# Keys, values and conv rows stored by channel, and a new order of steps, in a hybrid attention and DeltaNet decoder step

## The chip, the cores and the metric

The kernel runs on one core of a Trainium2 chip. The metric is the device time of one execution in microseconds. Five engines with their own instruction streams matter: TensorE (PE), VectorE (DVE), ScalarE (ACT), GpSimd (POOL), and SyncE (SP), which here only waits and issues DMAs.

## The reference

One layer of a decoder for 512 prompt tokens and 8 decode samples (one token each, 2048 tokens of past). All is float32.

```python
h = rmsnorm(x, g_pre)
q_a, k_a, v_a, z_a, qkv_b, z_b, beta, a = split(h @ w_in)      # 2048 -> 8208 columns
# mixer A, 8 heads x 128: partial rotary (first 32 dims) on q, k; softmax attention under
# (window, dilation) = (128,1), (512,4), (2048,16), the three merged by their denominators
# mixer B, 8 heads: causal conv of width 4 + SiLU on q/k/v, L2 norm, gated delta rule, per-head RMSNorm
gated = concat(o_a * silu(z_a), o_b * silu(z_b))               # 1024 + 1024
y = x + rmsnorm(gated @ w_out, g_post)
# outputs: y (prompt, sample); rotated keys and values of all new tokens; the last 3 conv input
# rows of the prompt; for each sample the old conv rows 1, 2 and the new one; delta states
```

New keys and values are small outputs that nothing else in the layer needs by token, except the values of the prompt, which the attention product takes with tokens on partitions.

## The kernel before

Everything is kept by channel: `h_hi` and `h_lo` hold the 2048 channels of the 520 tokens (512 prompt, 8 samples) as 16 blocks of 128 partitions. A float32 product is made of three products of a faster type: `w_hi h_hi`, `w_hi h_lo`, `w_lo h_hi` (L553 to L555). ACT rounds a weight block to `w_hi` (L954), DVE and POOL make `w_lo` (L1364, L1858), SP loads the next block into `w_raw` (L362) once `w_lo` of the block before it is there.

**Head stretches.** After two first tiles come eight stretches, one per head pair h, of eight projection tiles (q, k, v of mixer B's conv, its gate, then q, k, v, gate of mixer A). The first stretch is written out, the others are a loop; SP writes out the last as well. A tile is computed in two halves (256 and 264 tokens) of four quarters, so a stretch has 64 steps of 12 products. Between two steps every engine runs one step of each side task: Python generators, advanced in the order of a list (`step(work)`). `yield from idle(n)` sets the step at which a piece stands. So the order of each engine is fixed at build time by these numbers and by the order of the list. Side tasks are:
- `own_b`: conv of mixer B's q, k, v (DVE L1521 to L1534), its sigmoid (ACT L970 to L974), the product with it (DVE L1543, keys into `xk`, values into `xv`). The last 3 prompt columns and the 8 sample columns of the conv input `xq` are transposed on PE (L702), copied by ACT (L1178) and stored by two DMAs of ACT's queue.
- `own_a`: rotary on `xa`, `xk` (DVE L1460 to L1462); then PE transposes keys (L650), the sample columns of q and k (L651, L652), values (L657) and their sample columns (L658); ACT copies them to `ktok`, `qkrow`, `vtok`, `vrow` and stores them by token. `scratch_q` passes the sample queries to `qb`, the same row in every partition.
- `mix_b`, `mix_q`: the delta rule in chunks of 128. PE step 24 transposes keys (L715); ACT takes their norms; DVE makes the decay argument (L1554, L1555) and `b_kb` (L1563), which PE transposes at step 28 (L727). At the end PE transposes the output `b_o` (L802) after DVE's L1628.
- `delta_decode`: the samples' step of the delta rule.
- `tail_a(h - 1)`, `attn_decode(h - 1)`: prompt attention and sample attention of the head before. The latter: dot products of the cached keys with `qb` on DVE (L1718), their transposes on PE (L854), softmax on DVE, ACT, DVE (L1727 to L1731, L1269, L1735 to L1740), PE (L858, L860), scaling of the cached values on ACT (L1284), sums on DVE (L1743, L1746), column sums on PE (L865).

**After the last head** come 40 more steps with the output projection's first tiles (L887 to L889): each step is four blocks k of one half. Their input, the gated rows of the 16 head halves, was kept in DRAM (`scratch_g`) and is read back: rows 0 to 8 early, 9 to 14 by `late_rows`, in groups that share a semaphore (`ROW_GROUPS`). `splits(n)` names the rows that ACT (`g_hi`, L1311) and DVE (`g_lo`, L1767) split at step n: rows 8, 9 at n = 2, rows 10, 11 at n = 3. The tail and decode of the last head run in the same steps. Then a part follows in which DVE adds output tiles (L1799 to L1804), and then 11 plain tiles.

Of the kernel before, what the change touches and what calls it, by code (L numbers as in the profile page):

```python
# [6 lines left out]
F32 = mybir.dt.float32  # L7
# [5 lines left out]
P = 128  # L13
# [119 lines left out]
ROW_GROUPS = ((0, 1, 2, 3, 4, 5, 6, 8), (9, 10, 11), (12, 13, 14))  # L133
# [38 lines left out]
def build(nc, x_prompt, x_sample, cache_k, cache_v, state_conv, state_delta, g_pre, w_in, w_ba, conv_w, a_log, dt_bias,  # L172
          onorm_w, w_out, g_post, c_ident, c_upper, c_causal, c_levels, c_lnmask, c_rope,
          y_p, y_s, wk_p, wv_p, cv_p, st_p, wk_s, wv_s, cv_s, st_s):
    kp_v = wk_p[0, 0].rearrange("(c p) h d -> p c h d", p=P)
    vp_v = wv_p[0, 0].rearrange("(c p) h d -> p c h d", p=P)
    scratch_q = nc.dram_tensor("scratch_q", (NH, NB * HD), F32, kind="Internal").ap()
    scratch_g = nc.dram_tensor("scratch_g", (KT, P, TP), F32, kind="Internal").ap()

    with ExitStack() as ctx:  # L180
# [3 lines left out]
        def sem(name):  # L184
# [22 lines left out]
        ktok = mem[:, 15 * TP:16 * TP].rearrange("p (c d) -> p c d", c=NC)  # L207
# [44 lines left out]
        qkrow = rb[0:NB, 5 * P:7 * P].rearrange("p (n t) -> p n t", n=2)  # L252
        vrow = rb[0:NB, 7 * P:8 * P]
# [57 lines left out]
        def mx(n):  # L311
# [10 lines left out]
            "q_swap q_ok k_swap k_ok k_T ktok_ok k_out v_T vtok_ok v_out row_out qrow_out scores negmax expd "  # L322
# [4 lines left out]
            "zero_cols cw_ok crow_ps crow_ok crow_out conv_ok conv_sig kv_silu q_silu "  # L327
# [29 lines left out]
        def _(sp):  # L357
# [37 lines left out]
            sp.dma_start(cv_s[0, :, 0:2, :], state_conv[0, :, 1:3, :]).then_inc(s["S_out"], 16)  # L395
# [22 lines left out]
            def attn_decode(hh):  # L418
                yield from idle(8)
# [11 lines left out]
            def attn_rows(h):  # L431
# [9 lines left out]
                sp.dma_start(qb[:], scratch_q[h].partition_broadcast(P)).then_inc(s["qb_in"], 16)  # L441
# [25 lines left out]
            def early_rows():  # L467
# [3 lines left out]
                for k in (4, 5):  # L471
                    load_row(k)
# [45 lines left out]
            sp.wait_ge(s["h_lo_ok"], H_READY + KT + 2)  # L518
            for c in range(NC):
# [22 lines left out]
        def _(pe):  # L542
# [99 lines left out]
            def own_a(h):  # L642

                yield from idle(53)
                pe.wait_ge(s["k_ok"], h + 1)
                pe.wait_ge(s["d_add"], 2 * h + 2)
# [4 lines left out]
                pe.transpose(MD[0:NB, 1, 0:P], xa[:, TP:TT], ident[:])  # L651
                pe.transpose(MD[0:NB, 1, P:2 * P], xk[:, TP:TT], ident[:]).then_inc(s["k_T"], 1)  # L652
                yield from idle(6)
                pe.wait_ge(s["proj_sb"], 16 * h + 16)
# [1326 lines left out]
```

## Time and profile before

| | us |
|---|---|
| median of 3 runs | 1336.98 (1335.55 to 1337.41) |
| the profiled execution | 1335.67 |
| its span | 1333.8 |
| PE busy | 1255.9 (94%) |
| DVE busy | 768.1 (58%) |
| ACT busy | 543.2 (41%) |
| POOL busy | 288.6 (22%) |
| mean granted clock of PE | 0.988 |

Busy time of PE counts each product from its start to its end, and they overlap; so what an instruction costs is read from the starts of its neighbours. The granted clock is a share of 2.4 GHz. A difference between two times of this kernel below 0.2% can't be told from none.

### The profile page before, as it was taken

To read this page: it belongs to the slowest core of one execution; us is meant where nothing else is said; L and a number is where in the kernel's file an instruction comes from. 1 tells how busy PE (TensorE), PEld (TensorE's weight loads), DVE (VectorE), ACT (ScalarE), POOL (GpSimd) and SP (SyncE) were. 2 spreads that over 40 slices of the span, in tenths; PEclk is the share of its full clock that TensorE was granted. 3 is DMA by queue.
4 is the path that set the end of the run, shared out by engine and by line. 5 is a ranking of instruction groups with operands and counts; after the bars stand their busy time and mean duration, and the time that the engine had idled before them with its cause. 6 is when DMAs were issued, how large, how long until landed. Compare 5 with 4: busy or idle time off the path is not lost. (4 is left out here: it accounts for less than half of the span.)

```text
span 1333.8 us, 28478 instructions
## 1 busy us (share of the span) xinstructions
PE 1255.9 (94%) x10094; PEld 1208.7 (91%) x10094; DVE 768.1 (58%) x1872; ACT 543.2 (41%) x1472; POOL 288.6 (22%) x271
## 2 busy tenths in 40 slices
PE   4999998999999999999999999999999998899997
PEld 4989998999899989998999899989998997889996
DVE  6465377537653775376537753765377555474445
ACT  6353344434443444334433443344334544412210
POOL 1123212321232123112321231123212311122220
PEclk9999999999999999999999999999999998999999
DMA  7231434143424342434243424342434254312253
GB/s 227 90 96 50 145 108 140 61 142 101 130 66 140 98 135 66 138 103 129 64 140 100 133 66 138 105 127 65 138 100 150 66 184 130 110 64 94 94 190 129
DMA packets 82707, 151.90 MB, mean 114 GB/s; under 512 B 8793, under 2 KB 27330, under 8 KB 81026
## 3 DMA queue, kind: packets, MB, share of 16 engines
q1 hardware_dynamic: 72222, 144.87, 33.7%
q10 hardware_dynamic: 10384, 5.50, 1.6%
q8 instruction: 86, 1.41, 0.4%
q14 instruction: 15, 0.12, 0.0%
HBM read 132.20 MB, written 17.27 MB: 112 GB/s over the span
## 5 line engine op out<-in xcount | busy, mean ns | idle before, releaser
L553 PE MATMUL PJ<-h_hi,w_hi 128*128 128x264 f32 (+1 forms) x2432 | 722.4, 297 | 7.7 <-ACT memx L981 7.6
L554 PE MATMUL PJ<-h_lo,w_hi 128*128 128x264 f32 (+1 forms) x2432 | 688.2, 283 | 0.0
L555 PE MATMUL PJ<-h_hi,w_lo 128*128 128x264 f32 (+1 forms) x2432 | 686.6, 282 | 0.0
L553 PEld LDWEIGHTS PJ<-h_hi,w_hi 128*128 128x128 f32 x2432 | 461.0, 190 | 25.5 <-issue 12.4
L554 PEld LDWEIGHTS PJ<-h_lo,w_hi 128*128 128x128 f32 x2432 | 461.0, 190 | 2.8 <-issue 1.7
L555 PEld LDWEIGHTS PJ<-h_hi,w_lo 128*128 128x128 f32 x2432 | 459.2, 189 | 0.0
L1858 POOL TENSOR_TENSOR w_lo<-w_raw,w_hi 128x512 fp32r<-128x512 f32 x160 | 210.3, 1314 | 897.4 <-ACT w_hi L954 897.4
L954 ACT ACTIVATE w_hi<-w_raw 128x512 fp32r<-128x512 f32 x320 | 197.6, 624 | 103.2 <-PE PJ L555 84.1
L1364 DVE TENSOR_TENSOR w_lo<-w_raw,w_hi 128x512 fp32r<-128x512 f32 x160 | 114.0, 718 | 117.1 <-ACT w_hi L954 113.4
L981 ACT ACTIVATE memx<-PJ 128x264 f32<-128x264 f32 (+2 forms) x130 | 49.2, 380 | 68.4 <-PE PJ L555 57.0
L1223 ACT ACTIVATE mem<-MX 128x256 f32<-128x256 f32 x48 | 18.4, 384 | 116.1 <-PE MX L755 115.5
L1601 DVE TENSOR_TENSOR mem<-mem,MX 128x256 f32<-128x256 f32 (+1 forms) x48 | 18.9, 395 | 75.2 <-PE MX L774 75.2
L1523 DVE SCALAR_TENSOR_TENSOR memx<-memx,cw 128x512 f32<-128x512 f32 x72 | 60.4, 839 | 1.7
L887 PE MATMUL PJ<-h_hi,w_hi 128*128 128x256 f32 (+1 forms) x160 | 50.2, 314 | 7.9 <-DVE h_lo L1767 4.9
L1718 DVE CUSTOM_DVE_ANT_0 kv<-kv,qb 128x128 f32<-128x128 f32 x192 | 51.2, 323 | 0.0
L1907 POOL TENSOR_TENSOR mem<-mem,levels 128x256 f32<-128x256 f32 x48 | 38.8, 809 | 49.8 <-DVE mem L1576 22.0
L888 PE MATMUL PJ<-h_lo,w_hi 128*128 128x256 f32 (+1 forms) x160 | 47.2, 295 | 0.0
L889 PE MATMUL PJ<-h_hi,w_lo 128*128 128x256 f32 (+1 forms) x160 | 47.0, 294 | 0.0
L1801 DVE COPY memx<-PJ 128x256 f32<-128x256 f32 (+1 forms) x24 | 10.3, 428 | 63.0 <-PE PJ L555 61.8
L774 PE MATMUL MX<-mem 128*128 128x64 f32 x352 | 45.0, 269 | 0.0
L774 PEld LDWEIGHTS MX<-mem 128*128 128x128 f32 x352 | 43.1, 192 | 0.0
L1284 ACT ACTIVATE kv<-kv,pT 128x128 f32<-128x128 f32 x128 | 40.4, 389 | 4.5 <-issue 4.5
(317 smaller groups left out, 1618.4 us busy)
## 6 DMA issues: line engine op xcount, KB each, us to landing
w_raw<-in_w_in SPq DMA_DIRECT2D x256, 256.0 KB, 2.6
w_raw<-in_w_out SPq DMA_DIRECT2D x64, 256.0 KB, 2.8
kv<-in_cache_win_k SPq DMA_DIRECT2D x24, 512.0 KB, 3.5
kv<-in_cache_win_v SPq DMA_DIRECT2D x16, 512.0 KB, 3.5
mem<-in_x_prompt SPq DMA_DIRECT2D x4, 1024.0 KB, 10.1
S<-in_state_delta SPq DMA_DIRECT2D x8, 512.0 KB, 3.4
out<-S SPq DMA_DIRECT2D x8, 512.0 KB, 3.8
out<-mem ACTq DMA_DIRECT2D x16, 256.0 KB, 3.2
```

Of the source, the lines that this page charges most:

```text
L553: pe.matmul(out, wh, h_hi[:, k, tok], start=k == 0, stop=False)
L554: pe.matmul(out, wh, h_lo[:, k, tok], start=False, stop=False)
L555: last = pe.matmul(out, wl, h_hi[:, k, tok], start=False, stop=k == KT - 1)
L774: last = pe.matmul(blocks(mx(3)[:, c, :], n, c // 2), b_U[:, c, :], blocks(b_Y[:, c % 2, :], n, c // 2), start=True, stop=True)
L887: pe.matmul(out, wh, h_hi[:, k, tok], start=start and i == 0, stop=False)
L888: pe.matmul(out, wh, h_lo[:, k, tok], start=False, stop=False)
L954: act.activation(w_hi[:, par, 4 * q:4 * q + 4, :], w_raw[:, q, :, :], ACT.Copy).then_inc(s["w_hi_ok"], 1)
L981: act.activation(dst[:, o:o + WIDTH[half]], PJ[0:n, bank(T, half), 0:WIDTH[half]], ACT.Copy).then_inc(s["proj_sb"], 1)
L1364: dve.tensor_tensor(w_lo[:, par, 4 * q:4 * q + 4, :], w_raw[:, q, :, :], w_hi[:, par, 4 * q:4 * q + 4, :].bitcast(F32), ALU.subtract).then ...
L1523: link(dve.scalar_tensor_tensor(acc[:, 0:TP], xq[:, i:i + TP], w[:, 24 + i:25 + i], acc[:, 0:TP], ALU.mult, ALU.add))
L1718: last = dve.tensor_tensor_reduce(out=x, in0=x, in1=qb[:, b * HD:(b + 1) * HD], scale=1.0, scalar=0.0, op0=ALU.mult, op1=ALU.add, accum_ou ...
L1858: pool.tensor_tensor(w_lo[:, par, 4 * q:4 * q + 4, :], w_raw[:, q, :, :], w_hi[:, par, 4 * q:4 * q + 4, :].bitcast(F32), ALU.subtract).the ...
```

## The change

1. Keys, values, conv rows and sample queries are stored by channel, straight from `xk`, `xv`, `xq`, `xa`, by SP (`conv_out`, `attn_out`). The outputs of the program have other shapes; the host puts their axes in order. PE's transposes L650, L651, L652, L658 and L702 and ACT's copies and stores of them go. The transposes of the prompt's values stay, one step later. Guards on `xq`, `xk`, `xv` now wait for the stores.
2. On DVE, `mix_b` comes before `own_b` and `own_a` in the list of the loop.
3. In the loop, `attn_decode` runs its softmax part two steps later (`late=2`) on DVE, PE, ACT; the value scaling and the sums keep their steps.
4. Row 9 gets the place of `ktok` and is reloaded with rows 4 and 5. After the last head SP runs a step of its side tasks before the weight load of that step, not behind it.
5. The last head's `attn_decode` runs six steps sooner (`late=-6`) on all engines.

```diff
-ROW_GROUPS = ((0, 1, 2, 3, 4, 5, 6, 8), (9, 10, 11), (12, 13, 14))
+ROW_GROUPS = ((0, 1, 2, 3, 4, 5, 6, 8, 9), (10, 11), (12, 13, 14))
...
+            def conv_out(h):
+                yield from idle(9)
+                for j in range(3):
+                    sp.wait_ge(s["proj_sb"], 16 * h + (2 * j + 4))
+                    sp.dma_start(c_new[h, j], xq[:, TP:3 + TT]).then_inc(s["crow_out"], 16)
+                    yield from idle(8)
+            def attn_out(h):
+                yield from idle(46)
+                sp.wait_ge(s["q_ok"], h + 1)
+                sp.dma_start(scratch_q[h], xa[:, TP:TT]).then_inc(s["qrow_out"], 16)
+                yield from idle(7)
+                sp.wait_ge(s["k_ok"], h + 1)
+                sp.dma_start(k_new[h], xk).then_inc(s["k_out"], 16)
+                yield from idle(5)
+                sp.wait_ge(s["proj_sb"], 16 * h + 16)
+                sp.dma_start(v_new[h], xv).then_inc(s["v_out"], 16)
...
-                for k in (4, 5):
+                for k in (4, 5, 9):
                     load_row(k)
...
             def late_rows():
                 sp.wait_ge(s["gated_b"], NH)
-                for k in (9, 10, 11):
+                for k in (10, 11):
                     load_row(k)
                 yield
                 sp.wait_ge(s["v_T"], NH)
                 sp.wait_ge(s["stash_v"], NH)
+                sp.wait_ge(s["v_out"], 16 * NH)
                 for k in (12, 13, 14):
                     load_row(k)
...
-            work = [late_rows(), attn_decode(h)]
+            work = [late_rows(), attn_decode(h, late=-6)]
             for n in range(40):
+                step(work)
                 if n % 2 == 0 and n < 8 * PARTS:
                     slot, p = n // 8, n // 2 % 4
                     wait_lo(T_O + slot + 1, p)
                     load_out(slot + 2, p)
-                step(work)
...   PE
             def own_a(h):
-                yield from idle(53)
...
+                yield from idle(60)
+                pe.wait_ge(s["proj_sb"], 16 * h + 16)
                 if not isinstance(h, int) or h > 0:
                     pe.wait_ge(s["gated_ad"], h)
                 for c in range(NC):
-                    pe.transpose(MD[:, 0, c * P:(c + 1) * P], xk[:, c * P:(c + 1) * P], ident[:])
...
-            def own_b(h):
-                for j in range(3):
-                    yield from idle((11, 7, 8)[j])
...
-                    pe.transpose(MD[0:11, 1, 0:P], xq[:, 3 + TP - 3:3 + TT], ident[:]).then_inc(s["crow_ps"], 1)
...   ACT, guard of the copy into xq
                     act.wait_ge(s["conv_ok"], 3 * h + n)
-                    act.wait_ge(s["crow_ps"], 3 * h + n)
+                    act.wait_ge(s["crow_out"], 16 * (3 * h + n))
...   DVE
-                stretch(h, [tail_a(h - 1), attn_decode(h - 1, sums=(24, 4, 3)), own_b(h), own_a(h), mix_b(h), mix_q(h),
+                stretch(h, [tail_a(h - 1), attn_decode(h - 1, late=2, sums=(22, 4, 3)), mix_b(h), own_b(h), own_a(h), mix_q(h),
                             delta_decode(h)])
```

What moves on DVE, in the loop, around step 25: `memx<-memx,cw` are the conv of q, `mem<-MX,hg` and `mem<-mem,causal` the decay argument, the first `mem<-MX,sk` is `b_kb`. Before:

```order
L1364 TENSOR_TENSOR w_lo<-w_raw,w_hi 128x512
L1523 SCALAR_TENSOR_TENSOR memx<-memx,cw 128x512
L1523 SCALAR_TENSOR_TENSOR memx<-memx,cw 128x512
...
L1534 TENSOR_SCALAR memx<-memx 128x520
L1554 TENSOR_TENSOR mem<-MX,hg 128x512
L1555 SCALAR_TENSOR_TENSOR mem<-mem,causal 128x512
L1563 TENSOR_TENSOR mem<-MX,sk 128x512
```

In the changed kernel, whose lines have other numbers:

```order
L1325 TENSOR_TENSOR w_lo<-w_raw,w_hi 128x512
L1517 TENSOR_TENSOR mem<-MX,hg 128x512
L1518 SCALAR_TENSOR_TENSOR mem<-mem,causal 128x512
L1484 SCALAR_TENSOR_TENSOR memx<-memx,cw 128x512
L1484 SCALAR_TENSOR_TENSOR memx<-memx,cw 128x512
...
L1495 TENSOR_SCALAR memx<-memx 128x520
L1526 TENSOR_TENSOR mem<-MX,sk 128x512
```

The decay argument moved ahead of the end of the conv; the same instructions stand between the weight step and `b_kb`.

On PE at steps 59 and 60 of a stretch (`ident,memx` are transposes of values, `ident,mem` that of `b_o`). Before:

```order
L555 MATMUL PJ<-h_hi,w_lo 128x256
L657 MATMUL MD<-ident,memx 128x128 [waits ktok_ok,proj_sb]
L657 MATMUL MD<-ident,memx 128x128 x3
L658 MATMUL MD<-ident,memx 8x128
L802 MATMUL MX<-ident,mem 128x128 [waits o_n]
L802 MATMUL MX<-ident,mem 128x128 x3
L553 MATMUL PJ<-h_hi,w_hi 128x264 [waits proj_sb]
```

And now:

```order
L797 MATMUL MX<-ident,mem 128x128 [waits o_n]
L797 MATMUL MX<-ident,mem 128x128 x3
L568 MATMUL PJ<-h_hi,w_hi 128x264 [waits proj_sb]
...
L570 MATMUL PJ<-h_hi,w_lo 128x264
L664 MATMUL MD<-ident,memx 128x128 [waits proj_sb]
L664 MATMUL MD<-ident,memx 128x128 x3
```

The value transposes moved from ahead of `b_o` to 12 products behind it.

On SP after the last head (`w_raw` are weight loads, `mem` and `memx<-scratch_g` the gated rows, `kv` cached keys). Before:

```order
L362 DMA w_raw<-in_w_out 128x512 [waits w_lo_dve]
L465 DMA mem<-scratch_g 128x512 [waits gated_b]
L465 DMA mem<-scratch_g 128x512 x2
L465 DMA mem<-scratch_g 128x512 [waits stash_v,v_T]
L465 DMA memx<-scratch_g 128x512 x2
L362 DMA w_raw<-in_w_out 128x512 [waits w_lo_pool]
```

And now:

```order
L479 DMA mem<-scratch_g 128x512 [waits gated_b]
L479 DMA mem<-scratch_g 128x512
L356 DMA w_raw<-in_w_out 128x512 [waits w_lo_dve]
L479 DMA mem<-scratch_g 128x512 [waits v_out,stash_v,v_T]
L479 DMA memx<-scratch_g 128x512 x2
L511 DMA out<-small 128x128
L415 DMA kv<-in_cache_win_k 128x1024 [waits red]
L356 DMA w_raw<-in_w_out 128x512 [waits w_lo_pool]
```

Two rows stand ahead of the weight load that waits for DVE, and a load of cached keys, which waits for the first dot products, stands ahead of the next.

## Rows read from the trace of the kernel before

**Rows 1.** The page: busy time of TensorE and its share, the other engines beside it.

```profile
PE 1255.9 (94%) x10094; PEld 1208.7 (91%) x10094; DVE 768.1 (58%) x1872; ACT 543.2 (41%) x1472; POOL 288.6 (22%) x271
```

**Rows 2.** Waits of all engines (waiter, releaser: us in total, times, longest).

```profile
PE MX L727 <- DVE mem L1563: 19.6, 8, 2.6
...
ACT rb L1269 <- DVE ds L1731: 12.9, 8, 1.6
...
PE MD L854 <- DVE sc L1718: 5.9, 7, 0.8
...
PE PJ L887 <- DVE h_lo L1767: 4.9, 2, 3.8
...
PE MD L865 <- DVE kv L1746: 4.6, 1, 4.6
...
PE MD L858 <- DVE rb L1740: 4.4, 7, 0.6
...
PE PJ L887 <- DVE mem L1802: 2.9, 2, 2.0
```

**Rows 3.** Three stretches: busy us and (instructions) by engine, then granted clock, DMA share, GB/s.

```profile
350.00:360.00 10.00, 7.57 (x52) 7.54 (x52) 4.92 (x10) 5.40 (x12) 2.55 (x2) 0.83 0.29 90
1108.00:1119.00 11.00, 8.34 (x35) 6.50 (x35) 7.56 (x14) 3.95 (x10) 1.27 (x1) 0.69 0.22 80
1160.00:1170.00 10.00, 8.32 (x44) 8.32 (x45) 5.07 (x14) 2.02 (x5) 1.28 (x1) 0.66 0.13 37
```

**Rows 4.** Timeline of PE around one conv row: start us, us, instruction.

```profile
348.25 0.28 PE L555 MATMUL PJ<-h_hi,w_lo 128*128 128x256 f32 x1
348.37 0.27 PE L702 MATMUL MD<-ident,memx 128*11 128x128 f32 x1
...
348.60 0.27 PE L554 MATMUL PJ<-h_lo,w_hi 128*128 128x256 f32 x1
```

**Rows 5.** Timeline of PE at step 53 of the last head.

```profile
1079.53 0.60 PE L650 MATMUL MD<-ident,memx 128*128 128x128 f32 x4
...
1080.18 0.39 PE L781 MATMUL MX<-small,mem 128*128 128x128 f32 x2
```

**Rows 6.** Timeline of PE at step 59 of a head ([idle before <-releaser] last).

```profile
291.95 0.60 PE L657 MATMUL MD<-ident,memx 128*128 128x128 f32 x4
...
292.82 0.66 PE L802 MATMUL MX<-ident,mem 128*128 128x128 f32 x4 [0.15 <-DVE mem L1628]
```

**Rows 7.** Timeline of VectorE (DVE) ahead of `b_kb`, same head as rows 4.

```profile
346.55 0.69 DVE L1364 TENSOR_TENSOR w_lo<-w_raw,w_hi 128x512 fp32r<-128x512 f32 x1 [1.03 <-ACT w_hi L954]
...
350.85 0.69 DVE L1555 SCALAR_TENSOR_TENSOR mem<-mem,causal 128x512 f32<-128x512 f32 x1
...
351.72 0.69 DVE L1563 TENSOR_TENSOR mem<-MX,sk 128x512 f32<-128x512 f32 x1
```

**Rows 8.** Timeline of all engines before L715, same head.

```profile
339.07 0.43 DVE L1534 TENSOR_SCALAR memx<-memx 128x520 f32<-128x520 f32 x1
...
342.58 0.69 DVE L1543 TENSOR_TENSOR memx<-memx 128x520 f32<-128x520 f32 x1
...
344.22 0.49 PE L715 MATMUL MX<-ident,memx 128*128 128x128 f32 x3
```

**Rows 9.** DMA issues: KB each, median us from issue to landing.

```profile
mem<-scratch_g SPq DMA_DIRECT2D x8, 256.0 KB, 4.5
...
memr<-memx ACTq DMA_DIRECT2D x32, 32.5 KB, 2.1
```

**Rows 10.** Timeline of SyncE's queue after the last head.

```profile
1095.30 6.44 SPq L362 DMA_DIRECT2D w_raw<-in_w_out  x3
1101.78 2.21 SPq L465 DMA_DIRECT2D mem<-scratch_g  x4
```

**Rows 11.** Timeline of ScalarE (ACT) and PE at the end of the last decode.

```profile
1154.47 2.44 ACT L1284 ACTIVATE qb<-qb,pT 128x128 f32<-128x128 f32 x8
...
1161.68 3.48 PE L865 MATMUL MD<-ones,kv 128*128 128x1 f32 x16 [4.65 <-DVE kv L1746]
```

More of the change, by code:

```diff
@@ L416, in stretch, with attn_decode @@
                 over(work)
-            def attn_decode(hh):
-                yield from idle(8)
+            def attn_decode(hh, late=0):
+                yield from idle(8 + late)
                 sp.wait_ge(s["red"], 3 * hh + 1)
@@ L649, in own_a @@
                 for c in range(NC):
-                    pe.transpose(MD[:, 0, c * P:(c + 1) * P], xk[:, c * P:(c + 1) * P], ident[:])
[L651 to L654, printed above, removed]
-                pe.wait_ge(s["ktok_ok"], 2 * h + 2)
-                for c in range(NC):
-                    pe.transpose(MD[:, 0, c * P:(c + 1) * P], xv[:, c * P:(c + 1) * P], ident[:])
-                pe.transpose(MD[0:NB, 1, 0:P], xv[:, TP:TT], ident[:]).then_inc(s["v_T"], 1)
+                    last = pe.transpose(MD[:, 0, c * P:(c + 1) * P], xv[:, c * P:(c + 1) * P], ident[:])
+                last.then_inc(s["v_T"], 1)
             def tail_a(hh):
@@ L845, in delta_decode, with attn_decode @@
                               stop=True).then_inc(s["d_outer"], 1)
-            def attn_decode(hh, sums=12):
-                yield from idle(17)
-                pe.wait_ge(s["vtok_ok"], 2 * hh + 2)
+            def attn_decode(hh, late=0, sums=12):
+                yield from idle(17 + late)
+                pe.wait_ge(s["vtok_ok"], hh + 1)
                 pe.wait_ge(s["qkp"], hh + 1)
@@ L890, in unit @@
                 return last
-            work = [later(tail_a(NH - 1)), attn_decode(NH - 1)]
+            work = [later(tail_a(NH - 1)), attn_decode(NH - 1, late=-6)]
             for n in range(40):
@@ L1171, in own_b @@
             def own_b(h):
-                for j, m in enumerate((1, 2, 0)):
-                    yield from idle((11, 4, 5)[j])
-                    act.wait_ge(s["crow_ps"], 3 * h + j + 1)
-                    if j > 0 or not isinstance(h, int) or h > 0:
-                        act.wait_ge(s["crow_out"], 32 * (3 * h + j))
-                    act.activation(rows, MD[0:11, 1, 0:P], ACT.Copy).then_inc(s["crow_ok"], 1)
-                    yield
+                for j in range(3):
+                    yield from idle((12, 5, 6)[j])
                     act.wait_ge(s["conv_ok"], 3 * h + j + 1)
@@ L1261, in delta_decode, with attn_decode @@
                     s["d_rows_ok"], 1)
-            def attn_decode(hh, lag=0, gap=0):
-                yield from idle(18)
-                act.wait_ge(s["row_out"], 16 * hh + 16)
-                act.wait_ge(s["qrow_out"], 16 * hh + 16)
-                act.wait_ge(s["v_out"], 32 * hh + 32)
+            def attn_decode(hh, late=0, lag=0, gap=0):
+                yield from idle(18 + late)
                 act.wait_ge(s["sc_max"], hh + 1)
@@ L1323, in _ @@
             g_hi_samples(0, KT - 1)
-            work = [later(tail_a(NH - 1)), attn_decode(NH - 1)]
+            work = [later(tail_a(NH - 1)), attn_decode(NH - 1, late=-6)]
             for n in range(40):
@@ L1708, in bt_s, with attn_decode @@
                 return dd[:, 12 - n, :]
-            def attn_decode(hh, sums=(9, 1, 4)):
-                yield from idle(7)
+            def attn_decode(hh, late=0, sums=(9, 1, 4)):
+                yield from idle(7 + min(late, 0))
                 dve.wait_ge(s["qb_in"], 16 * hh + 16)
+                q = qb[:].rearrange("p (d b) -> p b d", b=NB)
                 for n in range(3):
@@ L1723, in attn_decode @@
                     last.then_inc(s["red"], 1)
-                yield
-                yield
+                yield from idle(2 + max(late, 0))
                 dve.wait_ge(s["sc_T"], hh + 1)
@@ L1777, in _ @@
             g_lo_samples(0, KT - 1, 5)
-            work = [later(tail_a(NH - 1)), attn_decode(NH - 1)]
+            work = [later(tail_a(NH - 1)), attn_decode(NH - 1, late=-6)]
             for n in range(40):
@@ L1979 @@
     r = run_bass_kernel_spmd(nc, [arrays], core_ids=[0])
[L1980 removed]
+    return tuple(np.ascontiguousarray(a) for a in outputs(*(r.results[0][f"out_{i}"] for i in range(len(_OUTS)))))
```

99 lines of the change are left out of this document (34 added, 65 removed).

## The prediction

> **What bounds the kernel now.** I read the page's engine shares first. TensorE (PE) is busy in 94% of the span [rows 1], and no other engine is above 58%, so an edit is worth what it takes off PE's own instruction stream, or off a wait that PE really sits in. The list of waits comes second [rows 2]: PE's waits inside the eight head stretches are 19.6 us before the transpose of `b_kb` (L727, 2.45 on average, in each of 8 heads), 5.9 before L854 and 4.4 before L858 (7 heads each, decode softmax of the head before). After the stretches come 4.9 for `h_lo`, 4.6 for L865 and 2.9 for L1802. Third is the granted clock [rows 3]: it falls from 2.4 to 1.2 GHz after such waits. In 350 to 360 us the mean is 0.83, so 10 x 0.17 = 1.7 us are lost; three of the eight heads (3, 5 and 7) show this fall. In 1108 to 1119 it is 11 x 0.31 = 3.4 us, in 1160 to 1170 also 3.4. So the rest of the prediction asks, for each edit, whether PE then arrives earlier at the next wait or really finishes earlier.
>
> **Transposes that go.** Ten per head: three of conv rows (L702), four of keys and two of decode rows (L650 to L652), one of the decode value row (L658). Their busy time is no price, since PE overlaps them: around L702 the product two places on starts at 348.60 where it would have started 0.236 after 348.25 without it, at 348.49, so one costs 0.11 us [rows 4]. The six of step 53 take from 1079.53 to 1080.18, 0.65 us [rows 5]. All 80 are 8 x (0.65 + 0.44) = 8.7 us of stream. How much is kept depends on what PE meets next.
> - The six of step 53: nothing that PE waits for follows within the next steps, all 0.65 is kept. 8 x 0.65 = 5.2 us.
> - The value row and the four value transposes stood directly ahead of L802 and covered its wait for `b_o`. PE starts them at 291.95 and L802 at 292.82, still with 0.15 idle [rows 6]. The end of that wait is set by DVE and ACT, counted from L798. In the changed order L802 comes first and the value transposes one step (12 products) later. So L802 ends where it ended, the row's 0.11 buys nothing, and four transposes are paid anew: 4 x 0.11 plus about 0.08 for the broken stream, 0.52 per head, 4.2 us lost. Bounds: 0 (if `b_o` is ready earlier) and 0.87 - 0.15 = 0.72 per head.
> - The conv rows of steps 11, 18 and 26 lie in the stretch where DVE is behind PE (below). I give them nothing; the bound is 24 x 0.11 = 2.6 us.
>
> **"Mixer steps lead" on DVE.** L727 waits for L1563. The order rows show what the lead does: L1554 and L1555 now come before the last conv pieces instead of behind them, but L1563 is a step later and keeps all of the same work ahead of it. From the weight step at 346.55 DVE runs without a gap to L1563's end at 352.41 [rows 7]; a permutation of that row of instructions ends at the same time. The wait stays. It even grows by the 0.11 of the conv transpose that PE no longer runs in between, and by the 0.2 of the small ACT copy `pT`, which now comes in front of the weight copy that DVE waits for: 8 x 0.3 = 2.4 us more idle, of which 0.9 is only the saving that isn't kept. Net 1.5 us lost. What does come earlier is ACT's L1215, and PE waits for nothing behind it. I leave three clock falls in heads as they are; from none to eight they are worth -5 to +8.5 us.
>
> **Decode softmax two steps later.** L854 then finds its sums ready: 0.84 x 7 = 5.9 us gone. But DVE is the late one there, and what it owes is shifted. Before: conv end (L1534) at 339.07 to 339.50, then six small softmax operations, the weight step, and the value product L1543 from 342.58 to 343.27, with PE's L715 free to start at 344.22 [rows 8]. After: L1534 is 1.2 us earlier (the five L1727 to L1731 operations come behind it, to 339.3), ACT follows with its sigmoid, the exponentials and the weight copy until about 341.1, DVE with the weight step (341.8), the six softmax operations (343.05) and L1543 (343.75). L858 and L860 (0.45 us) now stand right ahead of L715. So PE would reach L858 at about 342.1, wait till 343.1, and start L715 at about 343.8: 0.4 us earlier than before, not the 0.84 + 0.62 that the two waits add up to. 7 x 0.4 = 2.8 us; bounds -0.3 (nothing but the two columns' cost) and 1.5 per head. ACT loses 24 small copies and eight pairs of large and small ones; PE's stream waits for none of them.
>
> **SP's new DMAs.** Six small or medium stores per head move from ACT's queue to SP's (0.33 us of issue each) and stand among weight loads. None of the values they wait for is later than the `w_lo` that SP has just waited for, so the loads behind them are late by about 2 us in a head where each has a tile (11 us) to spare. New is that `xq` may be overwritten only when its store has landed. The tightest store stands at step 17 and the overwriting copy on ACT at step 20, three steps of 12 x 0.118 = 1.4 us [rows 4], 4.2 us, against 2.1 us to landing for a 32.5 KB copy and 4.5 for a 256 KB row [rows 9]. I price it at 0 (bounds 0 to 1 us per head; PE asks for that copy some four steps later).
>
> **After the last head.** Here is the gain. Rows 9 to 14 leave SP at 1101.78, behind the last of three weight loads, which waits for DVE [rows 10], and PE stands 3.8 and 1.1 us for their `h_lo` [rows 2]. In the changed order row 9 comes with the early ones and rows 10, 11 leave before that load, at about 1098 (the load before it and 0.5 of issue), and land near 1102.5 by the 4.5 us of such rows [rows 9]; PE asks for them from 1106 on. The waits go (4.9 us), and the fall of the clock goes (3.4 us) [rows 3]. The first dot products of the last decode now sit on DVE between rows 7 to 11 (8 x 0.21 = 1.7 us), so about 1 us of new small waits comes back. The last decode itself: ACT scales values until 1156.91, DVE adds till 1161.6, and PE, out of other work for 4.65 us, runs L865 at half clock (3.48 us instead of 1.7) [rows 11]. Six steps sooner and with a chain that starts about 8 us sooner, I get by the same durations: dots done 1119.6, L854 at step 11, L858 at 1129.6, ACT's scaling 1130.4 to 1140.4, sums by 1144, and step 28 of PE ends at 1147.3. The wait goes (4.6), L865 takes 1.7 (1.8 saved), and the next 2.8 us of products at half clock give back 1.4. Sum: 4.9 + 3.4 + 4.6 + 1.8 + 1.4 - 1.0 = 15.1 us. Bounds: 8 us (only the rows' waits and their clock, less the dots) and 18 (with the 2.9 us before L1802 as well).
>
> **Sum.** 5.2 - 4.2 - 1.5 + 2.8 + 15.1 = 17.4 us, from 1335.67 us of the profiled execution (span 1333.8, 1.9 around it): 1318.3. The median of the runs shown (1336.98) is 1.3 above that execution, so 1319.5.
>
> **Rivals.**
> - *Slower: the softmax ahead of the value product holds every head.* L1543 now stands behind operations that wait for ACT's exponentials, and L715, the weight step and L1563 stand behind L1543. If ACT takes `p_exp` later than I laid out (it now lies behind two sigmoid passes), L715 is late in each of seven heads, and its idle time brings the clock down each time (1.7 us). For it: PE waits for DVE at two places of this stretch already. Against: ACT stood idle 12.9 / 8 = 1.6 us before that very operation [rows 2]. It decides from 17.4 / 7 = 2.5 us per head lost against the forecast, or from 1.3 us with falls in all eight heads; with 1.9 us and the falls it is 1319.5 + 13.3 + 8.5 = 1341.
> - *Half of the tail.* The dots between the row splits, or V loads that wait for `red`, hold PE up again and the clock falls once more: 8 instead of 15.1, 1326.6. For it: DVE, ACT and SP are all denser there than anywhere before. Falls of the clock in all eight heads alone end at 1328.
> - *The transposes count in full.* `b_o` is ready earlier, or PE is late enough everywhere that conv rows, value row and moved values cost and give as listed: 8.7 us where the forecast keeps 5.2 - 4.2 - 1.5 = -0.5: 1310.3.
> - *The lead does what its name says*, L727's wait vanishes with its clock falls: 19.6 + 5 us more than forecast, 1295. Against it stands the row of instructions itself. A rule of the Trainium skill comes out in the same place: "TensorE: Matmul & The Clock Gate", Part 4, counts about 275 ns for a transpose in a kernel. By that rule 80 are 22 us, 22.5 more than the forecast, and the sum would be 1297; the trace agrees with it as a duration (272 ns), while the starts lie 0.11 us apart.
>
> **How the numbers follow.** Forecast 0.55 (own range 1313 to 1323), full transposes 0.13, half of the tail 0.17, the lead 0.07, slower rival 0.08. The range 1307 to 1327 holds the first three but for their edges and leaves out some 0.16. A difference of 0.2% is what a measurement of this kernel can tell. Faster by more: 0.91; the slower rival splits into 0.03 within 0.2% and 0.06 slower.
>
> **What would show it.** Right: PE's wait before the `b_kb` transpose is still there, 2.5 to 2.9 us in eight heads; the wait before the `b_o` transpose grows from 0.15 to about 0.7; no wait before the scores' small transposes; no PE gap between the stretch's end and the first projection tile's third part; the last value sums end before PE's step 28. Wrong: heads (132.9 us apart now, from the first L802 to the last) shorter by over 1.5 us or longer by over 0.5; the wait for `b_kb` below 1 us; a new wait of PE for `h_lo` above 2 us.

## The result and the profile after

The changed kernel takes 1344.99 us (median of 4 runs, 1344.43 to 1345.91) against 1336.26 of the kernel before in the same comparison: a ratio of 1.0064 with a 95% interval of 1.0045 to 1.0083. It is slower, and 25.5 us above the forecast of 1319.5. The profiled run has a span of 1342.8.

The first view is the mean clock, one row of each kernel. By an estimate, 1342.8 x 0.019 = 25.5 us are lost to the lower level after and 1333.8 x 0.012 = 16.0 before; the part of it that falls into PE's own waits costs nothing.

```profile
core 0: 1333.8 us, clock 0.988
```

```profile
core 0: 1342.8 us, clock 0.981
```

The next view splits both spans at the first and the last transpose of `b_o` (L802 before, L797 after). In a row stand the length, the busy time with its instructions of PE, PEld, DVE, ACT and POOL, the clock, DMA share and GB/s.

```profile
161.70:1092.20 930.50, 894.20 (x7227) 859.43 (x7228) 549.68 (x1407) 406.98 (x1156) 212.08 (x204) 0.99 0.35 111
1092.20:1333.80 241.60, 221.87 (x1729) 213.82 (x1727) 130.30 (x299) 64.05 (x136) 42.21 (x33) 0.95 0.35 121
```

```profile
160.10:1110.50 950.40, 899.82 (x7157) 866.49 (x7158) 573.73 (x1407) 393.05 (x1113) 215.10 (x204) 0.98 0.35 109
1110.50:1342.80 232.30, 217.82 (x1733) 210.83 (x1731) 134.35 (x299) 63.99 (x135) 43.19 (x33) 0.98 0.37 126
```

The seven distances between heads (from one `b_o` transpose to the next) grew by 19.9 us together (132.9 to 135.8 each). What follows the last head shrank from 241.6 to 232.3, by 9.3. DVE is busy 24 us more in the heads although it has the same 1407 instructions: some of them got slower. The waits of PE after, answering to [rows 2]:

```profile
PE MX L722 <- DVE mem L1526: 19.7, 8, 3.6
...
PE MD L853 <- DVE rb L1703: 12.7, 7, 1.8
PE PJ L568 <- ACT memx L976: 10.5, 8, 1.6
PE MD L849 <- DVE sc L1682: 6.8, 8, 1.9
PE MX L797 <- DVE mem L1591: 5.6, 8, 0.7
```

Two of before that [rows 2] leaves out:

```profile
PE PJ L553 <- ACT memx L981: 7.6, 7, 1.4
...
PE MX L802 <- DVE mem L1628: 1.2, 8, 0.2
```

The five waits of the heads are 19.6 + 5.9 + 4.4 + 7.6 + 1.2 = 38.7 us before, and 19.7 + 12.7 + 10.5 + 5.6 and 4.9 of L849's 6.8 (1.9 fall behind the heads) = 53.4 after: 14.7 more. The ten transposes give 7 x 1.1 = 7.6 back. The other 13 of the 19.9 us fit the clock: by the estimate above its loss grew by 9.5 in all, though the part behind the heads lost 241.6 x 0.05 = 12 before and 232.3 x 0.02 = 5 after, so the heads lost some 16 more.

The wait for `b_kb` (L722 now) is where it was. The one for `b_o` (L797) is 0.70 in each of 8 heads, as forecast. The scores' wait (L849) did not go, and that for `rb` (L853) is three times what it was. The waits for `h_lo` and for the last value sums [rows 2, 11] are gone. But 11.6 us behind the last `b_o` PE makes a new stop:

```profile
1121.69 0.39 PE L882 MATMUL PJ<-h_hi,w_hi 128*128 128x264 f32 x1 [2.33 <-issue]
```

"Issue" means that the trace names nothing that PE waited for. Most kernels below have this stop too, at 1.5 to 3.3 us, also the two without the new order behind the heads (1.7 and 1.8); the kernel before has none. Its cause stays open. Two further views name what made DVE slow. First one line of DVE, the dot products of the decode: minimum, median and maximum in ns.

```profile
L1718 DVE CUSTOM_DVE_ANT_0 kv<-kv,qb x192: 276/283/1380, 183.1 to 1136.4; 128x128 f32<-128x128 f32 x192
```

```profile
L1682 DVE CUSTOM_DVE_ANT_0 kv<-kv,qb x192: 371/405/1510, 181.9 to 1142.3; 128x128 f32<-128x128 f32 x192
```

Second, the timeline of DVE and POOL ahead of L853, in the head of [rows 8], and a piece of the kernel before:

```profile
347.07 0.69 DVE L1325 TENSOR_TENSOR w_lo<-w_raw,w_hi 128x512 fp32r<-128x512 f32 x1 [1.86 <-ACT w_hi L949]
...
348.03 0.15 DVE L1700 RECIPROCAL ds<-ds 8x1 f32<-8x1 f32 x1
348.17 1.27 POOL L1819 TENSOR_TENSOR w_lo<-w_raw,w_hi 128x512 fp32r<-128x512 f32 x1 [10.01 <-ACT w_hi L949]
348.22 1.22 DVE L1701 TENSOR_TENSOR ds<-ds 8x1 f32<-8x1 f32 x1
...
349.48 0.22 DVE L1702 TENSOR_SCALAR dg<-ident,ds 8x8 f32<-8x8 f32 x1
349.62 0.40 DVE L1703 TENSOR_SCALAR rb<-rb,ds 8x384 f32<-8x384 f32 x1
...
350.07 0.38 PE L853 MATMUL MD<-dg,ones 8*128 8x8 f32 x2 [1.83 <-DVE rb L1703]
```

```profile
337.72 1.28 POOL L1858 TENSOR_TENSOR w_lo<-w_raw,w_hi 128x512 fp32r<-128x512 f32 x1 [6.03 <-ACT w_hi L954]
337.76 1.27 DVE L1531 SCALAR_TENSOR_TENSOR memx<-memx,cw 128x8 f32<-128x8 f32 x1
```

L1701 is a product of two 8x1 operands and takes 0.147 us elsewhere. Here it starts 0.05 us after POOL's `w_lo` and ends with it. In the kernel before, the POOL instruction of this stretch fell on L1531, a small piece of the conv ahead of these six operations.

### The profile page after: what moved, and what is told of

Same layout as the page of the kernel before. It is cut to its first block and busy times, and to the rows that moved or that the text cites. A ratio compares the mean times of both kernels' runs of the same rounds, so it can differ in the third digit from the quotient of the medians.

```text
span 1342.8 us, 28094 instructions
## 1 busy us (share of the span) xinstructions
PE 1255.2 (93%) x10014; PEld 1210.8 (90%) x10014; DVE 796.1 (59%) x1872; ACT 527.6 (39%) x1424; POOL 292.2 (22%) x271
## 2 busy tenths in 40 slices
DMA packets 80252, 151.80 MB, mean 113 GB/s; under 512 B 12945, under 2 KB 22834, under 8 KB 78578
## 3 DMA queue, kind: packets, MB, share of 16 engines
q10 hardware_dynamic: 1024, 1.07, 0.3%
## 5 line engine op out<-in xcount | busy, mean ns | idle before, releaser
L568 PE MATMUL PJ<-h_hi,w_hi 128*128 128x264 f32 (+1 forms) x2432 | 725.9, 298 | 10.5 <-ACT memx L976 10.5
L1819 POOL TENSOR_TENSOR w_lo<-w_raw,w_hi 128x512 fp32r<-128x512 f32 x160 | 214.7, 1344 | 890.7 <-ACT w_hi L949 890.7
L1682 DVE CUSTOM_DVE_ANT_0 kv<-kv,qb 128x128 f32<-128x128 f32 x192 | 76.6, 456 | 0.0
L965 ACT ACTIVATE memx<-memx 128x520 f32<-128x520 f32 x32 | 20.4, 636 | 138.4 <-DVE memx L1495 138.4
L1868 POOL TENSOR_TENSOR mem<-mem,levels 128x256 f32<-128x256 f32 x48 | 35.7, 743 | 58.1 <-DVE mem L1539 30.4
```

The lines of the kernel that those rows point to most:

```text
L568: pe.matmul(out, wh, h_hi[:, k, tok], start=k == 0, stop=False)
L1682: last = dve.tensor_tensor_reduce(out=x, in0=x, in1=q[:, b, :], scale=1.0, scalar=0.0, op0=ALU.mult, op1=ALU.add, accum_out=sc[:, n, b:b + 1])
L1819: pool.tensor_tensor(w_lo[:, par, 4 * q:4 * q + 4, :], w_raw[:, q, :, :], w_hi[:, par, 4 * q:4 * q + 4, :].bitcast(F32), ALU.subtract).the ...
```

## The experiments

A difference between two experiments is one of medians; where the intervals of their ratios overlap the text says so. The ratios are to the kernel before, run beside each (its medians were 1336.3 to 1338.6).

**Queries by token, written by the DMA itself.** The dot products read `qb[:].rearrange("p (d b) -> p b d", b=NB)`: 128 numbers, each 8 elements behind the last. That line stands in the change's code; my prediction gave it no term, and the diff above does not show it.

```diff
-sp.dma_start(scratch_q[h], xa[:, TP:TT])
+sp.dma_start(scratch_q[h].rearrange("(b d) -> d b", b=NB), xa[:, TP:TT])
...
-in1=q[:, b, :]
+in1=qb[:, b * HD:(b + 1) * HD]
...
```

> The changed kernel, but the sample queries lie by token in DRAM again, so that the dot products of the decode read qb with step 1 and not with step 8. Theory 1, the step: the 192 dots fall from 0.405 to 0.283 us, DVE is 24 x 0.12 = 2.9 us earlier in each head, the wait before L853 falls from 1.8 to under 0.8 us, the extra clock falls in the heads go, heads come down from 135.8 to about 132.5 us, the time to 1345.0 - 7 x 3.3 - 1 = 1321 (1316 to 1326). Theory 2, the order (softmax ahead of the value product, list order): DVE's dots get faster but DVE then waits for ACT in the same place, the wait before L853 stays near 1.8 us and the time stays above 1338.

Measured: 1370.18 (ratio 1.025, 1.0224 to 1.0275). Both theories missed. The dots fell to 0.285, but the store now consists of 1024 pieces of 4 bytes, and the small DMAs that swap the rotary rows were late:

```profile
DVE memx L1421 <- DMA memr<-memx: 39.0, 8, 8.0
...
PE MX L776 <- DVE small L1579: 24.4, 8, 5.9
```

DVE's rotary waits up to 8.0 us for the swapped rows of `xk`, and PE sits behind it at L776, where the changed kernel has no such wait. The two kernels derived from this one share that fault.

> As q_by_token, with the last decode at its old steps and SP's side tasks behind the weight load again (row 9 stays with the early rows). Theory 1 (the tail gains what its waits and clock falls show, 9 to 15 us): 9 to 15 us above q_by_token, near 1333, and the wait for the last value sums (4.6 us) is back. Theory 2 (the tail's gain is given back by DVE's denser steps): within 4 us of q_by_token.

Measured: 1376.98 (1.0282 to 1.0332), 6.8 above `q_by_token`; under the range of theory 1, over that of theory 2. It is measured again below without the fault.

> As q_by_token, with the softmax of the decode in the loop at its old steps (late=0, sums back). Theory 1 (my forecast's step: later is worth 0.4 us per head): 7 x 0.4 = 2.8 us above q_by_token. Theory 2 (the six operations ahead of the value product L1506 hold PE): 3 us or more below q_by_token, since the value product comes earlier. Theory 3 (DVE's work is only permuted): the same within 1.5 us.

Measured: 1360.74 (1.0144 to 1.0203), 9.4 below `q_by_token`: theory 2's direction. In the profiled executions the difference is 3.0 (1367.37 and 1364.39).

**The step alone, in the kernel before.** The dots read `in1=qb[:].rearrange("p (d b) -> p b d", b=NB)[:, b, :]`; nothing else differs.

> The kernel before, where only the dot products read qb with step 8; the scores are then made of the wrong elements, all else is computed as before. Theory 1: dots of 0.4 us, DVE 2.9 us later at the end of them, the waits before L854 and L727 grow by 2 to 3 us together in each head, with clock falls behind them: 1336.3 + 7 x 3 = 1357 (1350 to 1364). Theory 2: the dots have slack in the old order, under 0.5 us per head: 1336 to 1340.

Measured: 1353.24 (1.0128, 1.0103 to 1.0152), 16 us slower, by theory 1. The wait for the scores grew from 5.9 to 15.3 us and that for `b_kb` stayed; the clock (0.982) took some 8 more, by the same estimate.

```profile
PE MX L727 <- DVE mem L1563: 19.6, 8, 2.7
PE MD L854 <- DVE sc L1718: 15.3, 7, 2.2
```

**The step alone, in the changed kernel.** One line, so that the dots read with step 1.

```diff
-q = qb[:].rearrange("p (d b) -> p b d", b=NB)
+q = qb[:].rearrange("p (b d) -> p b d", b=NB)
```

> The changed kernel with nothing changed but the view through which the dot products read qb, step 1 in place of 8; the scores are then made of the wrong elements, and the store by channel and its DMA stay. Theory 1 (the reading step is the whole difference between the changed kernel and q_via_pe): dots of 0.283 us, 1329.3 - 0.9 (8 transposes of 0.11 less) = 1328.4 (1325 to 1331). Theory 2 (part of it was the DMA of the queries on SP's queue): 1335 or more.

Measured: 1333.35 (0.9956, 0.9935 to 0.9977). The step costs 11.6 us by the medians and 14 by the two ratios to the kernel before. The time is between the two theories.

**Queries by token through PE.** One transpose at step 53, one ACT copy, a store in full rows: 8 x 0.11 us of PE more, step 1, no pieces of 4 bytes. The main lines:

```diff
+pe.transpose(MD[0:NB, 1, 0:P], xa[:, TP:TT], ident[:])
...
+act.activation(rb[0:NB, 5 * P:6 * P], MD[0:NB, 1, 0:P], ACT.Copy)
...
+act.dma_start(scratch_q[h].rearrange("(b d) -> b d", b=NB), rb[0:NB, 5 * P:6 * P])
```

> The changed kernel, but the sample queries are transposed by PE at step 53, copied by ACT and stored by token in full rows, so that qb is read with step 1 and no DMA of 4-byte elements goes out. Theory 1 (step 8 is the whole loss): dots of 0.283 us, the wait before L722 and L853 back at their sum of before, 1321 (1316 to 1326). Theory 2 (two causes: step 8, and POOL's w_lo, which runs from 348.17 to 349.44 and keeps L1701 until it ends, in front of L853): the wait before the scores' small transposes stays at 1.8 us in each of 7 heads, only the wait for L976 (0.6 of 1.3 us) and a few clock falls go: 1332 to 1340.

Measured: 1329.34 (0.9945, 0.9923 to 0.9968). The time lies between the two ranges; the wait is theory 2's. That for `rb` is as it was after, 12.7 us:

```profile
PE MX L723 <- DVE mem L1538: 21.6, 8, 3.6
...
PE MD L855 <- DVE rb L1714: 12.7, 7, 1.8
```

This kernel has all the rest of the change, so what is left of the forecast's miss is read from it.

**Softmax at its old steps** (`late=0` in the loop on DVE, PE, ACT; the sums and the value scaling keep their steps), on `q_via_pe` and on the changed kernel.

> As q_via_pe, with the decode's softmax in the loop at its old steps. Theory 2 (there POOL's w_lo falls on conv pieces and not on the six small operations): the wait for rb falls from 1.8 to 0.6 us, 7 x 1.2 and clock falls less: 7 to 12 us below q_via_pe, near 1326. My forecast's step (later is worth 0.4 us a head): 2.8 us above q_via_pe. Theory 3 (a permutation): the same within 1.5 us.

> The changed kernel with the decode's softmax in the loop at its old steps, qb still read with step 8. Theory 2: the dots are late for L849 (wait 0.8 to 2.2 us, as in before_q_step8), the wait for rb falls to 0.6: both causes are of like size, so the time stays within 5 us of the changed kernel (1340 to 1348). If the six small operations were the larger cause by far, it falls below 1338; if step 8 alone counted, it rises above 1350.

Measured: 1326.42 (0.9912, 0.9881 to 0.9943), 2.9 below `q_via_pe`, and 1345.56 (1.0056), the same as the changed kernel. The second agrees with theory 2. The first has its direction at under half its price of 7 to 12, and the intervals of the ratios overlap; the two profiled executions differ by 0.4 us. So the time alone doesn't exclude theory 3. PE's waits in the heads even add up to the same: 21.6 + 12.7 + 6.2 = 40.5 us in `q_via_pe`, 27.2 + 7.4 + 5.1 + 1.2 = 40.9 here. What differs is where PE stands in a head. Its `b_o` and `b_kb` transposes in `q_via_pe`, then with the softmax at its old steps:

```profile
296.38 0.66 PE L798 MATMUL MX<-ident,mem 128*128 128x128 f32 x4 [0.70 <-DVE mem L1603]
357.85 0.66 PE L723 MATMUL MX<-ident,mem 128*128 128x128 f32 x4 [2.04 <-DVE mem L1538]
```

```profile
296.03 0.66 PE L798 MATMUL MX<-ident,mem 128*128 128x128 f32 x4 [0.70 <-DVE mem L1603]
356.38 0.65 PE L723 MATMUL MX<-ident,mem 128*128 128x128 f32 x4 [3.49 <-DVE mem L1538]
```

The distance is 61.47 us with the late softmax and 60.35 without, and within 0.03 the same in the next three heads; the key transposes between them stand 0.96 us later with it. The clock takes most of these 1.1 us back. Stretches of 10 us ahead of `b_kb` and behind it in `q_via_pe`, in the head above and in one with a longer wait:

```profile
347.50:357.80 10.30, 7.90 (x53) 7.61 (x53) 8.73 (x18) 4.58 (x19) 1.28 (x1) 0.83 0.37 125
357.80:368.00 10.20, 10.15 (x86) 10.16 (x86) 4.98 (x10) 3.98 (x8) 2.21 (x2) 1.00 0.21 64
613.40:623.70 10.30, 6.36 (x53) 6.07 (x53) 8.72 (x18) 4.58 (x19) 1.26 (x1) 0.95 0.40 123
623.70:634.00 10.30, 10.29 (x65) 10.29 (x66) 2.54 (x4) 3.34 (x7) 1.28 (x1) 0.72 0.17 63
```

Where the clock is down ahead of `b_kb` (0.83), PE arrives late at a wait that it would have anyway (2.04 us), and behind it the clock is at its upper level. Where it falls behind `b_kb` (0.72), PE has waited 3.56 us and the fall costs stream. Of the seven heads of the loop, `q_via_pe` has four of the first kind and three that wait 3.56 with the fall behind; with the softmax at its old steps all seven wait 3.5 and have it behind (1.00 ahead, 0.83 behind). What sets this stays open.

**Is it POOL?** The two small tensor_tensor operations as tensor_scalar; then POOL's `w_lo` of step 22 behind the softmax.

```diff
...
-dve.tensor_tensor(ds[:, 4:5], ds[:, 4:5], ds[:, 5:6], ALU.mult)
+dve.tensor_scalar(ds[:, 4:5], ds[:, 4:5], ds[:, 5:6], None, ALU.mult)
```

> As q_via_pe, with the two small tensor_tensor operations of the softmax's second part (sum and product, 8x1) written as tensor_scalar with the second number as a scalar operand. If POOL holds back only DVE operations with two tensors read from SBUF, L1701 falls from 1.22 to 0.15 us, the wait for rb from 1.8 to about 0.75, and the time by 7 x 1.07 to 7 x 1.07 + 6 (clock falls): 8 to 13 us below q_via_pe. If POOL holds back every DVE operation that starts while it runs, or the 1.07 us has another cause, nothing changes (within 1.5 us), or the wait moves to the next operation.

Measured: 1336.27 (0.9982, 0.9961 to 1.0003), 7 us slower (the intervals just overlap). DVE and POOL, with times from the start of the span:

```profile
347.08 1.26 POOL L1830 TENSOR_TENSOR w_lo<-w_raw,w_hi 128x512 fp32r<-128x512 f32 x1 [9.64 <-ACT w_hi L951]
...
347.19 0.20 DVE L1712 TENSOR_SCALAR ds<-ds 8x1 f32<-8x1 f32 x1
347.43 0.95 DVE L1713 TENSOR_SCALAR dg<-ident,ds 8x8 f32<-8x8 f32 x1
```

The product is held no more, but the next operation is, until POOL ends. The wait for `rb` fell from 1.81 to 1.57, and that for `b_kb` grew from 21.6 to 26.8 us. The mean clock is 0.980 against 0.988, some 11 us. Six heads wait 3.58 us for `b_kb` here, the second kind above, where `q_via_pe` has three; why a shift of 0.25 us brings that many, I can't say.

```diff
+if j == 2 and seg == 6 and not isinstance(h, int):
+    pool.wait_ge(s["p_norm"], h)
```

> q_via_pe, where POOL's w_lo of step 22 in the loop waits until DVE has made the last of the six small operations of the softmax. Theory 1 (POOL's operation holds DVE's L1712 for 1.07 us, and this is in front of PE): L1712 falls from 1.23 to 0.15 us, the wait for rb from 1.8 to 0.75, 7 x 1.07 and some clock falls: 1318 to 1323. Theory 2 (what is gained there is lost again at the next wait, b_kb, as with q_via_pe_one_input, since POOL then holds the conv pieces ahead of it): the wait for b_kb grows by as much, within 2 us of q_via_pe (1329.3), or slower.

Measured: 1326.65 (0.9913, 0.9892 to 0.9935), 2.7 below `q_via_pe`; the intervals overlap. L1712 is 0.147 in all 8 heads, so the 1.07 us are POOL's. The time is 0.7 below theory 2's range and 3.7 above theory 1's, and the waits are theory 2's:

```profile
PE MX L723 <- DVE mem L1538: 27.7, 8, 3.6
...
PE MD L855 <- DVE rb L1714: 5.1, 7, 0.8
```

7.6 us went from the wait for `rb` and 6.1 came back in front of `b_kb`. The transposes of `b_kb` do come earlier:

```profile
295.95 0.66 PE L798 MATMUL MX<-ident,mem 128*128 128x128 f32 x4 [0.70 <-DVE mem L1603]
356.29 0.66 PE L723 MATMUL MX<-ident,mem 128*128 128x128 f32 x4 [3.56 <-DVE mem L1538]
```

That is 60.34 us against 61.47, the same place as with the softmax at its old steps. So POOL's operation accounts for the whole 1.1 us that the two later steps cost there, and again the clock falls behind `b_kb` in all seven heads of the loop, which fits that only 2.7 us are left of 7 x 1.1.

**List order of before** (`mix_b` behind `own_b` and `own_a`), on `q_via_pe_late0`.

> q_via_pe_late0 with the list order of before on DVE (own_b, own_a ahead of mix_b). Theory 1 (my forecast: the lead only permutes DVE's row ahead of b_kb): the wait for b_kb stays near 3.4 us and the time within 2 us of q_via_pe_late0 (1326.4). Theory 2 (the lead has a cost of its own: POOL's w_lo now falls on a conv piece in front of b_kb, 1.0 us): the wait falls to about 2.4 us, and the time by 8 x 1 = 8 us and some clock falls, 1310 to 1318.

Measured: 1322.93 (0.9891, 0.9861 to 0.9920), 3.5 below; the ratios overlap, the waits don't: 27.2 us for `b_kb` with the lead, 20.5 without. The `b_kb` transposes stand 59.38 us behind those of `b_o` instead of 60.35. DVE and POOL with the lead, then without:

```profile
353.28 1.44 DVE L1504 SCALAR_TENSOR_TENSOR memx<-cw,memx 128x8 f32<-128x8 f32 x2
353.44 1.26 POOL L1830 TENSOR_TENSOR w_lo<-w_raw,w_hi 128x512 fp32r<-128x512 f32 x1 [5.96 <-ACT w_hi L951]
...
355.63 0.69 DVE L1538 TENSOR_TENSOR mem<-MX,sk 128x512 f32<-128x512 f32 x1
```

```profile
349.39 0.49 DVE L1504 SCALAR_TENSOR_TENSOR memx<-cw,memx 128x8 f32<-128x8 f32 x2
...
352.12 0.69 DVE L1538 TENSOR_TENSOR mem<-MX,sk 128x512 f32<-128x512 f32 x1
...
353.85 1.29 POOL L1830 TENSOR_TENSOR w_lo<-w_raw,w_hi 128x512 fp32r<-128x512 f32 x1 [8.92 <-ACT w_hi L951]
```

With the lead, ACT gets its decay argument sooner, so its weight copy and with it POOL's `w_lo` start sooner, and POOL lands on a conv piece (1.44 for two instead of 0.49) ahead of `b_kb`. Without, it comes behind `b_kb`. Theory 2 by its wait; the time is between the two ranges, at under half of theory 2's price.

**Value transposes at step 59.**

> q_via_pe_late0 with PE's four value transposes at step 59 again, directly ahead of those of b_o. My forecast's step (they cover the wait for b_o and are paid anew behind it): the wait for b_o falls from 0.70 to about 0.2 us, 8 x 0.5 = 4 us below q_via_pe_late0, 1322.5. Rival (their place is free, DVE sets the end of each head anyway): the same within 1.5 us.

Measured: 1321.85 (0.9883, 0.9855 to 0.9910), 4.6 below; the ratios overlap, and the wait for `b_o` is 0.26 in each head instead of 0.70. As forecast.

**The tail undone**, on `q_via_pe`.

> q_via_pe with the last decode at its old steps and SP's side tasks behind the weight load again (row 9 stays early). Theory 1 (my forecast's 15.1 us of the tail, of which row 9 alone is some 2): 9 to 15 us above q_via_pe, 1338 to 1345, with a wait for the last value sums near 4.6 us. Theory 2 (most of the gain is row 9 and the clock): within 5 us, up to 1334.

Measured: 1336.95 (0.9988, 0.9972 to 1.0005), 7.6 above, between the two ranges; 4.7 us of wait for the last value sums are back. A wait for `h_lo` is not, so the early place of row 9, which stays here, is enough to remove those 4.9 us. In the profiled executions the part behind the last `b_o` is 226.1 us with the edits (the row of `q_via_pe` below, at full clock) and 237.9 without. But 226.1 is the shortest of all: in the eleven profiled kernels with these edits and fast dots it goes up to 229.8, with 228.2 in the middle.

```profile
1098.40:1324.50 226.10, 214.39 (x1733) 206.10 (x1731) 130.03 (x299) 63.82 (x135) 43.11 (x33) 1.00 0.38 130
```

**`b_kb` sooner.** None of the above moves `b_kb` ahead of the conv's end. One `yield` does:

```diff
 dve.scalar_tensor_tensor(b_D, ...).then_inc(s["mix_arg"], 1)
-yield
 dve.wait_ge(s["mix_rs"], 2 * h + 1)
...
 dve.tensor_tensor(b_kdec, mx(0), ...)
+yield
 yield
```

> q_via_pe_late0, but DVE makes b_kb in the same step as the decay argument (step 25), ahead of the end of the conv, instead of one step later. Theory 1 (b_kb is late only because of the conv pieces and POOL's lock in front of it, 3.9 us): the wait of 3.4 us in each of 8 heads goes, and with it most clock falls in heads: 27 + 5 to 10 us below q_via_pe_late0, 1290 to 1297. Theory 2 (the conv then ends 1.5 us later and the wait turns up behind it, at ACT's sigmoid, at b_A or at the next b_o): half of it or less, 1310 to 1326.

> late0_kb_sooner with the value transposes at step 59 ahead of those of b_o (the two gains together). Theory 1, they add: 1310.8 - 4.6 = 1306 (1303 to 1309), the wait for b_o at 0.26 us. Theory 2, DVE sets the head's end anyway: 1310.8 within 1.5 us.

The first measured 1310.75 (0.9796, 0.9768 to 0.9823), 15.7 below `q_via_pe_late0`: the wait for `b_kb` is gone but in the written-out first head, and 15.1 us turned up behind it, two steps on, where PE waits for ACT's copy of the transposed `b_kb` (theory 2). The second, with the value transposes at step 59, measured 1302.91 (0.9734, 0.9712 to 0.9756), 7.9 further down, so the two gains add (theory 1, 0.1 under its range). In that comparison the kernel before took 1338.6, so it is 36 us faster, and the fastest of all. Its rows:

```profile
PE MX L729 <- ACT mem L1193: 15.2, 7, 2.2
...
PE MX L723 <- DVE mem L1537: 2.8, 1, 2.8
...
PE MX L798 <- DVE mem L1603: 2.1, 8, 0.3
```

```profile
162.00:1074.20 912.20, 881.12 (x7164) 849.71 (x7165) 549.34 (x1407) 394.90 (x1122) 212.59 (x204) 1.00 0.36 113
1074.20:1300.40 226.20, 213.36 (x1729) 205.46 (x1727) 129.42 (x299) 63.36 (x135) 43.19 (x33) 1.00 0.38 130
```

## Why the prediction was wrong

The steps of the prediction against what was measured, from the bottom of its sum:

- **The missing term.** DVE's 192 dots read `qb` with step 8 and take 0.405 us, not 0.283: 24 x 0.12 = 2.9 us more for DVE in each head. The prediction left this at nothing: it took the durations of DVE's row from the trace of before for operations whose operand had a new layout, in the heads and behind them (8 x 0.21 for the first dots of the last decode, which now start 0.34 us apart). Alone this costs 11.6 to 14 us in the changed kernel and 16 in the one before. A rule of the Trainium skill speaks of it: "SBUF — State Buffer", Door 1, says that a float32 operand may step by up to 4 elements for free and pays beyond. The measured 43% on the whole instruction at step 8 agree in sign; the Trainium skill gives no price for DVE there.
- **"L715 starts 0.4 us earlier", the softmax two steps later.** Forecast 2.8 us gained; measured 2.9 lost by medians whose intervals overlap. In the traces the key transposes stand 0.96 us later in each head, and those of `b_kb` 1.1. The prediction let L1735 to L1740 take 1.25 us by the rows of before. At their new step POOL's `w_lo` runs beside them and holds one for 1.07 us; with POOL behind them the 1.1 us are gone. The place was the slower rival's (the softmax in front of the value product), the mechanism not: that rival blamed ACT's exponentials, so that its 1341 lies near the 1345 measured is luck.
- **"A permutation of that row ends at the same time."** Forecast 1.5 us lost beside; measured 3.5 more by the lead (its ratios overlap), with `b_kb` 0.97 us later in each head. The sum of DVE's durations is not kept when the order changes, since it depends on what POOL does meanwhile. The Trainium skill, "SBUF — State Buffer", "SBUF: two separate sides", has the rule: DVE and GpSimd share one port pair under an exclusive lock; a DVE operation with two SBUF inputs or in a 2-port mode and a GpSimd operation block each other until the first has ended. The trace of before agrees (L1531 at 337.76 with 1.27 us for 0.23), and I read over it.
- **Value transposes behind `b_o`:** forecast 4.2 lost, measured 4.6 by medians (the ratios overlap), and 0.70 of wait, as said. Right.
- **The tail:** forecast 15.1, measured 11.8 to 15.5 from the last `b_o` to the end in eleven profiled kernels with fast dots, 13.4 in the middle (241.6 to 228.2). `q_via_pe` has the 15.5. In the changed kernel only 9.3 are left: the first dots with step 8 make PE wait 1.9 us for the scores, and the clock's mean there is 0.98 where `q_via_pe` has 1.00. Undoing the new order and the six steps moves the median by 7.6; row 9 stays early there, and its part was not tested alone. Right in place and somewhat too large; the new stop of 2.3 us had no place in it.
- **K, row and conv transposes:** 5.2 forecast, not tested alone.

By medians the second and third carry the forecast to `q_via_pe`: 1319.5 + 0.9 (its transposes) + 5.7 (from 2.8 gained to 2.9 lost) + 3.5 = 1329.6, measured 1329.3. That it comes out so closely is partly luck: the intervals overlap for both terms, the tail gave 13.4 in the middle for its 15.1, and the 5.2 us were not tested. From there back to the changed kernel it is -0.9 and 11.6, which gives 1340.0. The other 5.0 us stand in the difference between `after_read_step1` (1333.35) and the 1328.4 expected of it. The ratios of these two kernels overlap and differ by only 1.5 us. In their profiled executions the four waits of PE in the heads are 50.8 and 46.1 us, with 26.8 and 21.6 for `b_kb`: six heads against three of the kind whose clock falls behind `b_kb`. The mean clocks are 0.982 and 0.988. What decides where the clock falls stays open.

Of what the prediction said would show it: the wait for `b_o` and the end of the last value sums came out as it said, and that for `b_kb` stayed, though at 2.0 to 3.6 us and not 2.5 to 2.9. "No wait before the scores' small transposes" and "no PE gap" behind the last stretch did not (2.3 us, cause open), and "heads longer by over 0.5 us" was named as the sign of being wrong: they are longer by 2.8. A slip in its chances: the slower rival has 0.08 in one place and 0.03 + 0.06 in the other.

## What to carry to other kernels

When a change alters how data lies in memory, go through every reader of it and price its access pattern, even those that the diff touches in one word. Before a list of instructions on DVE is moved or called a permutation, lay POOL's instructions beside it, and look which one each will fall on. And where PE waits at several places for one engine's row, look at the last of them: what was saved at an earlier one can come back there, as a longer wait with a fall of the clock behind it.

## What the runs showed of the hardware

- A dot product of 128 elements on DVE took 0.283 us with step 1 and 0.405 with step 8 of one float32 operand.
- A POOL tensor_tensor of 1.27 us holds a DVE tensor_tensor that starts meanwhile, even one of 8x1 elements (0.15 to 1.23). It did not hold a tensor_scalar of 8x1 (0.20), but a tensor_scalar of 8x8 was held (0.22 to 0.95) and one of 128x512 too (0.49 to 1.39). So two tensor inputs are not the only case. The 0.95 is from `q_via_pe_one_input`, the 1.39 from `pool_behind_softmax`.
- With a store of 4 KB in pieces of 4 bytes, DVE waited up to 8 us for small DMAs of another queue, in all three kernels that have it and in none without. "DMA: Bandwidth & Descriptors", "Rules for kernel authors", of the Trainium skill says that a last dimension with gaps becomes one descriptor per element; the trace agrees, the packets under 512 bytes rose from 12945 to 20113, by 8 x (1024 - 128).
- The same wait of PE cost more or less by where the clock fell: 2.04 us with a mean clock of 0.83 in the 10 us ahead and 1.00 behind, 3.56 us with 0.95 ahead and 0.72 behind, in heads of one execution of `q_via_pe`.
